# One stream of weights, three places for the same work: regrouping the modulation and the mixers' small matmuls in a two-block transformer kernel

## The reference

```python
m_lat = jnp.split(s_lat @ w_ada[li] + b_ada[li], 6, axis=-1)      # modulation, sequence
m_ctx = jnp.split(s_ctx @ w_ada[li] + b_ada[li], 6, axis=-1)      # modulation, context
h  = rms_norm(x, g_mix[li]) * (1.0 + m_lat[1]) + m_lat[0]
hc = rms_norm(ctx, g_mix[li]) * (1.0 + m_ctx[1]) + m_ctx[0]
p, pc = h @ w_in[li], hc @ w_in[li]                               # 9 groups of 256 columns
y = concat(fourier_mix(p[:G]), diff_attention(p[G:4G], ...), na_attention(p[4G:7G], ...), chunk_gmlp(p[7G:], ...))
x = x + m_lat[2] * (y @ w_out[li])                                # and the same for ctx in layer 0
h = rms_norm(x, g_ffn[li]) * (1.0 + m_lat[4]) + m_lat[3]
x = x + m_lat[5] * conv_ffn(h, ...)                               # and the same for ctx in layer 0
```

## Time and profile before

| | |
|---|---|
| median of 3 runs | 3277.39 us (3271.11 to 3277.59) |
| profiled execution | 3273.77 us |
| its span in the trace | 3272.0 us |
| mean granted TensorE clock | 0.972 |
| PE busy | 3098.2 us, 95% |
| DVE, ACT, POOL busy | 1319.4, 742.9, 542.3 us |
| moved by DMA | 337.66 MB, mean 103 GB/s |

### The profile page before, as it was taken

How to read it: one execution, slowest core, us unless ns; L and a number is a source line. 1 busy time by engine, 2 the same in 40 slices (tenths; PEclk the granted TensorE clock), 3 DMA queues, 4 the chain that set the end, 5 groups by cost and what they waited for, 6 DMA issues and landing times.

```text
span 3272.0 us, 39252 instructions
## 1 busy us (share of the span) xinstructions
PE 3098.2 (95%) x15593; PEld 2342.5 (72%) x15593; DVE 1319.4 (40%) x2198; ACT 742.9 (23%) x1413; POOL 542.3 (17%) x445
## 2 busy tenths in 40 slices
PE   7989999999989899999979999999999998999999
PEld 4546478888655788644469888844488887698888
DVE  1045368772224343255456656532245322223100
ACT  2034121110123231134234444421000001221100
POOL 1000035554100000000022222100145442011000
PEclk9989999999998999999989999999999998999999
DMA  6228412222316443334300000121222223211343
GB/s 238 77 77 319 183 65 90 91 91 90 103 64 252 148 154 141 141 130 166 142 7 14 14 14 14 46 90 65 77 78 88 80 90 107 90 40 43 148 144 116
DMA packets 51808, 337.66 MB, mean 103 GB/s; under 512 B 6304, under 2 KB 7968, under 8 KB 12608
## 3 DMA queue, kind: packets, MB, share of 16 engines
q1 hardware_dynamic: 47088, 323.05, 27.4%
q10 hardware_dynamic: 2976, 7.14, 0.6%
q0 software_dynamic: 1584, 5.21, 0.5%
HBM read 334.26 MB, written 1.11 MB: 102 GB/s over the span
## 4 chain that ended last, share of the span: by engine, by line
PE 83%; issue 9%; ACT 4%; DVE 2%; DVEq 0%; ACTq 0%; DMA 0%; POOL 0%; POOLq 0%
PE psum L208 29%; PE psum L2482 24%; PE psum L229 3%; PE psum L304 3%; PE psum L1425 3%; PE psum L1407 2%; PE psum L2051 2%; PE psum L371 2%; PE psum L242 1%; PE psum L1416 1%; ACT h_sb L887 1%; PE psum L398 1%; ACT arena L1680 1%; PE psum L1463 1%; PE psum L1486 1%
## 5 line engine op out<-in xcount | busy, mean ns | idle before, releaser
L208 PE MATMUL psum<-h_sb,ring 128*128 128x256 f32 (+1 forms) x2560 | 792.0, 470 | 16.5 <-ACT h_sb L887 16.4
L208 PEld LDWEIGHTS psum<-h_sb,ring 128*128 128x128 f32 x2560 | 484.9, 191 | 312.6 <-issue 266.3
L208 PE MATMUL psum<-arena,ring 128*128 128x256 f32 (+1 forms) x1504 | 418.1, 442 | 16.9 <-DVEq L716 7.5
L208 PEld LDWEIGHTS psum<-arena,ring 128*128 128x128 f32 x1504 | 291.9, 194 | 144.1 <-issue 92.5
L2482 PE MATMUL psum<-arena,ring 128*128 128x256 f32 x1168 | 267.4, 379 | 0.0
L2482 PEld LDWEIGHTS psum<-arena,ring 128*128 128x128 f32 x1168 | 221.9, 190 | 30.2
L2482 PE MATMUL psum<-h_sb,ring 128*128 128x256 f32 x912 | 216.6, 387 | 8.6 <-ACT h_sb L887 8.5
L2482 PE MATMUL psum<-arena,c 128*128 128x256 f32 x888 | 205.2, 379 | 1.8 <-DVE arena L2520 1.2
L1730 POOL TENSOR_TENSOR ring<-c,gates 128x512 f32<-128x512 f32 x32 | 32.6, 1041 | 1026.9 <-PE psum L208 797.2
L2482 PEld LDWEIGHTS psum<-h_sb,ring 128*128 128x128 f32 x912 | 174.2, 193 | 39.8 <-ACT h_sb L887 8.6
L2482 PEld LDWEIGHTS psum<-arena,c 128*128 128x128 f32 x888 | 168.5, 190 | 25.8 <-DVE arena L2520 2.0
(11 more groups left out here) (311 smaller groups left out, 4240.9 us busy)
## 6 DMA issues: line engine op xcount, KB each, us to landing
ring<-in_stream SPq DMA_DIRECT2D x302, 1024.0 KB, 4.8
arena<-decays SPq DMA_DIRECT2D x24, 256.0 KB, 3.6
x_sb<-in_x ACTq DMA_DIRECT2D x1, 2048.0 KB, 17.5
arena<-in_rpb POOLq DMA_DIRECT2D x32, 64.0 KB, 5.3
arena<-in_c POOLq DMA_DIRECT2D x1, 1120.0 KB, 7.9
x_sb<-in_ctx ACTq DMA_DIRECT2D x1, 1024.0 KB, 7.0
c<-in_c ACTq DMA_DIRECT2D x1, 1024.0 KB, 4.9
out<-x_sb POOLq DMA_DIRECT2D x1, 1024.0 KB, 5.0
```

The costliest lines, as they stand in the source:

```text
L208: ins = pe.matmul(out_ap, lhs(k), rhs(k), start=first and k == 0, stop=last and k == nk - 1)
```

## The change

1. **Batched modulation.** `silu_w` becomes wider (62 columns per block instead of 32, zero but for two), and the window of 32 columns slides, so that each ada chunk of a batch adds its two rows into another row pair of the same bank. ACT copies and PE turns once per batch (9 batches of 4 to 16 chunks), not once per chunk.
2. **Other places for the chunks.** 8 before layer 0 as before; 16 two by two behind the projection chunks of layer 0 (`ada_in1`); 22 and 17 in the two attentions (40 and 24 before); 2, 4, 3, 4 in `gap1` to `gap4`, around the sums of norms 1 to 4 (`GAP_AHEAD` of them before the sums); 20 in `ada_last` (24 before).
3. **First norm.** The condition vector is loaded by a transfer of its own, ahead of all others of its queue; PE no longer waits for the constants; DVE adds the squares, and two matmuls sum them after the 8 ada chunks. Norms 0 and 2 go stream by stream (`BY_STREAM`).
4. **Mixers' work behind the projection's chunks.** `IN1_ORDER` brings u and v of the gMLP forward. `pe_slot`, called after each chunk of the projection, makes the small products that `pe_mixers1` made at the end; `act_slot` and the new order of `dve_mixers1` do the same for ACT and DVE.
5. **Around the norms.** `act_norm` copies its gap's batch before its table load. `dve_mods` of layer 1's modulation moves into the first FFN, that of the second block's into the second FFN. Norms 4 and 6 come ahead of the transfers of constants. The two sets of `w_sums` change places.

```diff
-ADA_PARTS = {"ada_first": (0, MIX_ADA), "ada_next0": (MIX_ADA, 2 * ADA_CHUNKS),
-             "ada_next1": (2 * ADA_CHUNKS, 3 * ADA_CHUNKS), "ada_last": (3 * ADA_CHUNKS, 4 * ADA_CHUNKS)}
+QKV_TURNS = 8
+QKV_ADA = [3] * 4 + [2] * 4
+ADA_PARTS = _spans([("ada_first", MIX_ADA), ("ada_in1", 16), ("ada_next0", 22), ("gap1", 2), ("gap2", 4),
+                    ("ada_next1", 17), ("gap3", 3), ("gap4", 4), ("ada_last", sum(QKV_ADA))])
+GAP_AHEAD = {"gap1": 2, "gap2": 0, "gap3": 1, "gap4": 2}
+ADA_BATCHES = [(0, 8), (8, 24), (24, 36), (36, 48), (48, 52), (52, 62), (62, 72), (72, 84), (84, 96)]
+TURNED_AT_END = ("ada_first", "gap1", "gap3", "ada_last")
...
+BY_STREAM = (0, 2)
+IN1_ORDER = (0, 7, 8, 1, 2, 4, 5, 3, 6)
...
         def pe_ada(pe, name, i):
             n, a = ada_at(name, i)
-            if a == 0:
-                pe.wait_ge(S["silu_ready"], 1)
-            elif i > 0:
-                pe_turn(pe, a - 1)
+            batch, q, last = ada_batch(a)
+            if a > 0 and q == 0 and a not in [ADA_PARTS[part][1] for part in TURNED_AT_END]:
+                pe_turn(pe, batch - 1)
...
+        def pe_ada_first(pe):
+            pe.wait_ge(S["silu_ready"], 1)
+            for i in range(MIX_ADA):
+                pe_ada(pe, "ada_first", i)
+            pe_norm_sums(pe, 0, TOK)
+            pe.wait_ge(S["silu_ready"], 2)
+            pe_turn(pe, 0)
...
         def act_ada(act, name, i):
             n, a = ada_at(name, i)
+            batch, _, last = ada_batch(a)
+            if not last:
+                return
             act.wait_ge(S["products"], 2 * (n + 1))
...
         def pe_norm_sums(pe, k, cols):
+            gap = f"gap{k}"
+            if gap in ADA_PARTS:
+                for i in range(GAP_AHEAD[gap]):
+                    pe_ada(pe, gap, i)
...
+            if gap in ADA_PARTS:
+                for i in range(GAP_AHEAD[gap], ada_count(gap)):
+                    pe_ada(pe, gap, i)
+                if gap in TURNED_AT_END:
+                    pe_turn(pe, ada_batch(ADA_PARTS[gap][1] - 1)[0])
...
+                if li == 0 and c < IN1_CHUNKS - 1:
+                    for i in range(2):
+                        pe_ada(pe, "ada_in1", 2 * c + i)
+                pe_slot(pe, li, c)
+
+        def pe_slot(pe, li, c):
+            if c in (1, 2):
...
+                dft_n = c1("dft_n", 1024).rearrange("p (t c) -> p t c", t=2)
+                for n in ((0, 1, 2) if c == 1 else (3,)):
...
+            if c == 3:
+                pe.wait_ge(S["f_copied"], 3 * li + 2)
...
+            if c == 4:
+                pe.wait_ge(S["gm_ready"], 2 * li + 1)
+                pe.wait_ge(S["f_copied"], 3 * li + 3)
...
+            if c == 5:
+                pe.wait_ge(S["gm_ready"], 2 * li + 2)
+                pe.wait_ge(S["qk_sq"], 3 * li + 1)
+                for n in range(3):
+                    ins = pe_qk_sum(pe, n, 4 + n)
...
+            if c == 6:
+                pe.wait_ge(S["qk_rinv"], 3 * li + 1)
+                pe.wait_ge(S["qk_sq"], 3 * li + 2)
...
+            if c == 7:
+                pe.wait_ge(S["qk_rinv"], 3 * li + 2)
+                pe.wait_ge(S["qk_normed"], li + 1)
...
         def pe_mixers1(pe, li):
-            if li == 0:
-                pe.wait_ge(S["loaded_c1"], 32)
             pe.wait_ge(S["bank_free"], sched[f"1in{li}"][1] + 2 * IN1_CHUNKS)
-            for half in range(2):
-                pe.wait_ge(S["qk_sq"], 2 * li + half + 1)
...
             pe.wait_ge(S["qk_ready"], li + 1)
             pe_attention(pe, li, UNITS[li], U0[li])
...
-        def act_norm(act, use, l, part, norm=None, streams=2):
+        def act_norm(act, use, l, part, norm=None, streams=2, mods=None):
+            if f"gap{norm}" in ADA_PARTS:
+                act_ada_all(act, f"gap{norm}")
             if norm is not None:
                 act_log_exp_set(act)
                 act.wait_ge(S["n_sum"], norm + 1)
...
+            dve_mods(dve, 1, "b_ada1", 0, 48)
+            dve_gain(dve, 1, 0, "g_mix1")
+            dve_gain(dve, 1, 1, "g_ffn1")
+            dve.drain().then_inc(S["mods_ready"], 1)
...
-            act.dma_start(vec[:, :], t["vec"]).then_inc(S["loaded_vec"], 16)
+            act.dma_start(vec[:, 0:4 * KT], t["vec"][:, 0:4 * KT]).then_inc(S["loaded_c"], 16)
             act.dma_start(ident[:, :], t["ident"]).then_inc(S["loaded_vec"], 16)
+            act.dma_start(vec[:, 4 * KT:], t["vec"][:, 4 * KT:]).then_inc(S["loaded_vec"], 16)
...
-            pe.wait_ge(S["loaded_vec"], 48)
...
+        b["act_norm"](act, 4, 2, 0, 4, mods=4)
         act.wait_ge(T["arena_free"], 1)
         act.dma_start(self.c2[:, 0:CD["end"]], t["c_delta"]).then_inc(T["loaded_c2"], 16)
...
-            act.wait_ge(S["mods_ready"], 4)
+            act.wait_ge(S["mods_ready"], 5)
+            b["act_norm"](act, 6, 3, 0, 6)
             act.wait_ge(T["arena_free"], 2)
             act.dma_start(self.c2[:, :], t["c2"]).then_inc(T["loaded_c2"], 16)
```

More of the change, by code:

```diff
@@ L51, in _offsets, with _spans @@
     return out
+def _spans(counts):
+    at, out = 0, {}
+    for name, count in counts:
+        out[name] = (at, at + count)
+        at += count
+    return out
 VEC_SIZES = [("c", 4 * KT)]
@@ L173, in build_program, with ada_count @@
         sched = {}
+        def ada_count(name):
+            first, end = ADA_PARTS[name]
+            return end - first
         def plan(name, chunks, results):
@@ L228, in pe_ada, with ada_batch @@
                     k = 4 * half + j
-                    ins = pe.matmul(bank(7)[32 * j:32 * (j + 1), 0:256], silu[:, a // (2 * ADA_CHUNKS), k, :],
-                                    w[:, n % RING, k, :], start=half == 0, stop=half == 1)
+                    ins = pe.matmul(bank(7)[32 * j:32 * (j + 1), 0:256],
+                                    silu[:, a // (2 * ADA_CHUNKS), k, ADA_ROWS - 2 - 2 * q:2 * ADA_ROWS - 2 - 2 * q],
+                                    w[:, n % RING, k, :], start=q == 0 and half == 0, stop=last and half == 1)
                 ins.then_inc(S["products"], 1)
+        def ada_batch(a):
+            batch = [a < end for _, end in ADA_BATCHES].index(True)
+            first, end = ADA_BATCHES[batch]
+            return batch, a - first, a == end - 1
         def turned(l, m0=0, m1=48):
@@ L897, in dve_norm @@
                 dve.wait_ge(S["n_rinv"], norm + 1)
+            if norm in BY_STREAM:
+                for n, (kt, s) in enumerate(norm_order(norm, streams)):
+                    part = slice(s * SEQ, (s + 1) * SEQ)
+                    ins = dve.tensor_tensor(h[:, kt, part], x[:, kt, part], rinv[:, part], ALU.mult)
+                    if n % streams == streams - 1:
+                        ins.then_inc(S["n_normed"], 1)
+                return
             for kt in range(KT):
@@ L2723, in _constants2, with layout_second @@
                  for m in (tri + strict + pair, tri + span[0] + span[1], strict + pair))
-def layout_second(i, stream, out):
+def layout_second(i, stream, out, ada):
     dn = i["dn_w_in_2"][0]
-    qkv, ada = _chunks(dn[:, :4096]), _chunks(i["ada_w_2"][1])
-    for j in range(QKV_CHUNKS // 2):
-        stream.append(np.stack([qkv[2 * j], ada[3 * j], qkv[2 * j + 1], ada[3 * j + 1], ada[3 * j + 2]]))
+    qkv, ada = _chunks(dn[:, :4096]), ada[slice(*ADA_PARTS["ada_last"])]
+    for j in range(QKV_TURNS):
+        m = sum(QKV_ADA[:j])
+        stream.append(np.stack([qkv[2 * j], ada[m], qkv[2 * j + 1], *ada[m + 1:m + QKV_ADA[j]]]))
     stream.append(_chunks(dn[:, 4096:6144]))
@@ L2847, in layout @@
     if BLOCKS == 2:
-        layout_second(i, stream, out)
+        layout_second(i, stream, out, ada)
     out["stream"] = np.concatenate(stream)
```

390 lines of the change are left out of this document (216 added, 174 removed).

## The result

The changed kernel takes 3176.12 us, the median of 4 runs (3175.33 to 3176.84), against 3274.49 us of the kernel before on the same chip (3271.11 to 3277.59, 4 runs): a ratio of 0.970, interval 0.9683 to 0.9717. One execution of a later experiment, pool_sum_early, took 4388.29 us at a granted clock of 0.676 and is counted nowhere. The forecast was 3168 us, 8 us too low, within its range. The profiled execution has a span of 3175.1 us against 3272.0.

A forecast was written before the change was run, and what follows sets the result against it. PE was taken to run densely except at the start, the two mixer layers and the norms. Terms summing to -109.5 us on the profiled 3273.8 gave 3164.3, plus 3.6 for the median: 3168 us, range 3152 to 3186.

The forecast's parts named there:

- attention 0 and 1: Both attentions, with fewer ada chunks and turns: 131.4 to 93.5 us (-37.9) and 85.5 to 60.5 us (-25.0).
- layer 1's small products: Stretch behind layer 1's projection, its work moved between the chunks: 42.1 us becomes 22.9, -19.2.
- rival b: Mixer projections: slots don't hide the hand-overs, PE waits in order; +31 us and cold work +8, 3207; chance 0.08.
- rival c: Layer 0's projection with small products: its 148 us of work runs at half rate and doubles, 3316 us; chance 0.03.
- Rival a: Attentions stay paced by hand-overs, 4.07 and 3.0 us a turn: 113 and about 64 us, +23, 3191; chance 0.15.
- DVE's floor of 3.30 a turn: Attention 0, turns without an ada chunk: DVE's 3.30 us exceeds PE's 2.54, in the context 2.4 against 1.45; +4.3 us.
- The start: Up to the first projection chunk's end: PE starts at some 7 us, DMA sets the pace, end at 52.0; -17.4 us.
- 3 to 4 us of short steps: At the start, from the last two sums through turn, bias, gain, Ln and Exp to ACT's first h at 35.4.
- Norm 1: ACT's copy and table load come after two ada chunks, +0.7 us; POOL's later second sum costs nothing.
- Norm 2: ACT's copy waits for four ada chunks before table load and Ln, +6.9; stream order gives back; +5.0 in all.
- Norm 4: Earlier table load saves 2.5, two ada chunks before the sums cost 1.5, two after fill a hole; -2.5 us.
- The delta rule's projection: Four ada chunks fewer, 4.0, and turns at some 0.42 us each, less one that stays, 9.3; -13.3 us.

The follow-up runs named there:

- pool_sum_early: The changed kernel with POOL's first sum of weights of the first FFN before the norm and its second held until h is complete: 3173.57 us.
- batch_alone: The kernel before with batched modulation in 8 batches and nothing else, its chunks in their old places: 3224.34 us, ratio 0.9842.
- extra_turn: The changed kernel with two more small matmuls in every turn of both attentions: 3216.59 us, median of 2 runs, ratio 0.9824.
- norms_by_row: The changed kernel with norms 0 and 2 by row blocks again, both streams of each, as in the kernel before: 3175.43 us.
- act_copy_late: The changed kernel with ACT's copy of the gap's batch behind the reciprocal root at norms 1 and 3, behind h at norm 2: 3169.93 us.
- three_in_gap2: act_copy_late with three ada chunks instead of four in norm 2's gap, the fourth moved into attention 1: 3162.35 us, ratio 0.9655.
- gap4_two: The changed kernel with two of norm 4's four ada chunks moved into the delta rule's projection: 3175.8 us.
- changed_again: The changed kernel as it is, timed again in the last series: 3176.79 us.
- four_edits: three_in_gap2 and gap4_two together, with POOL's first sum early and its second after DVE's first four sums: 3157.84 us, ratio 0.9643.

## Why the prediction was right, and where its terms were off

**The mechanism was right.** Three terms carry the gain, attention 0 and 1 and layer 1's small products: -82.1 forecast, -83.8 measured. The slots hide the hand-overs between PE, ACT and DVE (rival b did not occur), and the mixture in the projections ran at granted clock 1.00 (rival c did not either). Rival a, attentions that keep the old pace, is refuted by attention 0's 93.33 us, against 113 by that rival, and by the chain's turn of 2.54 us without an ada chunk. Of the 98 us some 51 come from batching alone, by batch_alone.

**Attention 0: right size, one step wrong.** I set 93.5 (its terms as written make 93.2), with 4.3 us for DVE's floor of 3.30 a turn in turns where PE needs 2.54. DVE does have more work than PE in such a turn, but PE does not wait for it. DVE's first instruction in three turns running, the first without an ada chunk:

```profile
218.00 1.23 DVE L594 TENSOR_REDUCE small<-psum 128x2 f32<-128x1024 f32 x1 [0.41 <-PE psum L489]
...
221.06 1.21 DVE L594 TENSOR_REDUCE small<-psum 128x2 f32<-128x1024 f32 x1
...
224.34 1.23 DVE L594 TENSOR_REDUCE small<-psum 128x2 f32<-128x1024 f32 x1
```

DVE takes 3.06 us for the first turn without going idle. The next scores end at 220.49, so it comes to them 0.57 us late. The next two turns have an ada chunk, which makes them 3.54 us long for PE; at 227.63 DVE is only 0.06 us behind the scores again. PE is busy without a gap from 212.37 to 253.76 us. The step that failed is the one that charges each short turn by itself: DVE may fall behind in one turn and catch up in the next, and only the mean over the turns counts. extra_turn shows PE binding. What takes the 4.3 us in its place is idle time, 3.3 us in all, and the clock at the entry, 0.67 from 203.5 to 212 us.

**The start, -14.6 and not -17.4.** The byte count held: 11.0 MB, at 423 to 424 GB/s from 3 us on. PE ended the last ada chunk at 32.05 and DVE its squares at 31.81, where I had 29.5 and 31.4, so the sums begin 0.6 us late. The term that was mis-sized lies behind them: "3 to 4 us of short steps" from there to ACT's first h. It took 5.9 us, 31.98 to 37.84 (forecast 35.4), and the two sums are most of it:

```profile
31.98 1.83 PE L325 MATMUL psum<-h_sb,ones 128*128 128x512 f32 x2
...
33.61 1.91 PE L327 MATMUL psum<-h_sb,ones 128*128 128x512 f32 x2
```

They take 3.54 us at a granted clock of 0.54; the same sums of norm 1 take 1.12 and 1.02 us. Waiting for loads had left PE busy for 13.38 of the 26 us before 31 us.

The Trainium skill (DMA: Bandwidth & Descriptors, Specifications) gives about 358 GB/s as one core's half of what a stack of HBM gives. On the one core that runs here the trace goes beyond it, with 424 GB/s over the stretch from 3 to 5 us and 423 from 5 to 31.

**Norm 1, +4.5 and not +0.7.** The step that failed is "POOL's second sum waits for a turn at some 422 and is needed 20 us later: nothing". I asked when its result is needed, and not beside what it runs. Nor did I see that the first sum waits for the use of the chunk before it in the stream, which is now an ada chunk of the gap: it begins at 363.36, 1.4 us after the output projection's end, where it began 13.4 us ahead of that end before (403.97 against 417.38). pool_sum_early shows that this is the whole: 15.56 again, and nothing of the +0.7 that I had for ACT's copy and table load.

The Trainium skill (SBUF — State Buffer, Who interferes with whom) says that a DVE instruction with two inputs in SBUF contends with a GpSimd instruction that reads SBUF, and that the ports the two share are an exclusive lock. By that rule, and the durations of this case, strict turns would take 0.61 + 1.27 = 1.88 us a pair, an estimate. The trace agrees for the most part: one multiplication every 1.67 us (ACT's pairs of L1010 start at 370.16, 371.83 and 373.51) beside POOL's instructions of 1.53 us.

**Norm 2, +5.0 as forecast, in part by luck.** The steps are in the timeline, but their sizes were off and made up for each other. Ln comes 8.01 us after the last sums begin (783.37 to 791.38) and not 1.95 (834.35 to 836.30): +6.1, where I had +6.9. The order by stream gave back 1.1 us (18.9 to 17.8 from ACT's first h to the chunk's end) and not 2.5; norms_by_row says 1.1 too. And 6.9 less 2.5 is 4.4, not the 5.0 of the sum. What I did not see is the bound behind it, the ring, which act_copy_late uncovered and three_in_gap2 removed.

**Norm 4, +1.4 and not -2.5.** From the down projection's end to ACT's first h it took 6.64 us before (1352.49 to 1359.13) and takes 5.77 now (1267.27 to 1273.04): the table load's 2.5 less the two ada chunks' 1.5, about as forecast. The step that failed is "two after fill a hole and keep the clock up", which the other 1.5 us of the -2.5 stood for: from ACT's first h to PE's first record 1.23 us became 3.49, and the first four records took 3.78 us. Each chunk of 1.05 MB takes 2.5 us to load at 416 GB/s, and PE had used three by 1271.79, 4.4 us after the first; I had counted PE's time for them and not the stream's. With gap4_two the stage is 7.00, -0.9 against before.

**The delta rule's projection, -10.7 and not -13.3.** The term of turns was mis-sized, 0.42 us each by the earlier trace rows and 0.37 by batch_alone's 7.4 / 20, and the count was off for the stage as it is cut here: between the projection's first and last record lie 22 ada chunks and 21 turns before, 19 and 1 after, so three chunks and 20 turns go, not four and 22 or 23. (Of those behind the last record, 4.84 us became 4.29.) So 7.4 and 3 chunks of 1.0 make 10.4 of the 10.7. The first 32 records behind norm 4 took 0.5 us longer than before, the other way, so some 0.8 us stay unexplained.

**Two terms that were not there at all.** Layer 1's output projection is 1.5 us longer, and the last stage 1.6. The second is not the change's: in changed_again it is 495.81 and not 499.04. The first is the clock: the same 132 records take 37.69 us at a granted clock of 0.91 before and 39.22 at 0.87 after. It is 39.2 to 39.4 us in five more executions, but 37.86 at 0.91 in pool_sum_early, whose edit does not touch it, and 36.24 at 0.95 in four_edits. What sets the clock there stays open.

## What to carry to other kernels

Work that is put into a gap uses more than PE's time there: count how many slots of the weight ring it takes, because a gap of as many chunks as the ring has slots turns into a wait for DMA and a cold clock behind it; three chunks in a ring of four left no wait for the stream here, and a fourth made the stage 5.4 us longer, to save 1.0 elsewhere. When an engine off the critical path gets another start time, look at what it then runs beside, not only at when its result is needed. And before calling an engine the floor of a loop, compare its work with the bounding engine's over several turns: one turn in which it has more to do is made up for in the next, if it may fall behind.

## What the runs showed that I had not expected

**DVE and POOL slow each other.** With float32 sums and products out of SBUF on both: DVE's 128 x 512 products, eight in 11.70 us and not 4.91; its 128 x 1024 sums 2.12 us and not 1.23; POOL's 128 x 512 1.53 to 2.25 us and not 1.27.

**Steps of 1 to 4 us between executions of equal code.** Attention 1 took 60.15 or 62.85 us over the executions with 17 ada chunks, attention 0 93.3 to 96.4, the last stage 496 or 499. Attention 1 with 18 ada chunks in three_in_gap2 and in four_edits, where its instructions are the same:

```profile
916.40:977.50 61.10, 59.77 (x536) 35.09 (x536) 39.70 (x89) 26.09 (x65) 0.00 (x0) 1.00 0.86 321
```

```profile
911.90:975.60 63.70, 62.85 (x536) 36.10 (x536) 39.95 (x88) 26.08 (x65) 0.00 (x0) 0.95 0.84 308
```

The same 536 records, at granted clock 1.00 and 0.95. The second block between its first projection and norm 6 took 1117.1 us in the changed kernel and in changed_again, and 1113.2 in act_copy_late, three_in_gap2 and four_edits, with the same 5841 records. So part of what these three gain in total is not their edits'. What sets the clock stays open; it means that an edit worth 1 to 4 us has to be read from its stage's records, not from the total.
